# Last convolution group of a streaming encoder chained by channel halves, and one GpSimd scaling moved behind two copies

## What is computed

```python
h = rmsnorm(x, norm_g)
proj = h @ w_in
# attention with band and sinks, gated linear attention (GLA), convolution; each times its gate
u = cv * jax.nn.sigmoid(cgl)
c = conv_lax(concat(conv_hist, u), conv_w) + conv_b            # depthwise, width 31, 256 channels
c = jax.nn.silu(layernorm(c, ln_g, ln_b)) @ w_pw + b_pw
y_conv = c * jax.nn.silu(cg)
y = concat([y_attn, y_gla, y_conv]) @ w_out
return x + y, ...
```

## Time and profile before

| | |
|---|---|
| median of 3 runs | 925.39 us (924.95 to 925.93) |
| profiled execution | 925.71 us, of which the span shown is 923.9 us |
| PE busy | 890.1 us (96% of the span) |
| DVE busy | 784.4 us (85%) |
| ACT busy | 481.6 us (52%) |
| POOL busy | 215.7 us (23%) |
| mean granted TensorE clock | 0.994 |

### The profile page before, as it was taken

How to read it: one execution, slowest core, us unless ns; L and a number is a source line. 1 busy time by engine, 2 the same in 40 slices (tenths; PEclk the granted TensorE clock), 3 DMA queues, 4 the chain that set the end, 5 groups by cost and what they waited for, 6 DMA issues and landing times. The chain is left out here.

```text
span 923.9 us, 15888 instructions
## 1 busy us (share of the span) xinstructions
PE 890.1 (96%) x5655; PEld 800.9 (87%) x5655; DVE 784.4 (85%) x1896; ACT 481.6 (52%) x1182; POOL 215.7 (23%) x259
## 2 busy tenths in 40 slices
PE   6889999999999999998999999999999999999997
PEld 5778888888888888876898888889999899998985
DVE  7898888888888888889879999888788969788994
ACT  7787666666676766668663261341515124142231
POOL 1432222222222222223022231311202012120310
PEclk9999999999999999999999999999999999999999
DMA  9553323222333333135451221121130312204021
GB/s 303 190 191 115 103 82 115 96 110 84 111 106 111 114 115 103 70 120 145 119 160 52 76 69 64 52 81 57 38 101 1 100 39 69 70 3 135 1 81 60
DMA packets 58062, 88.04 MB, mean 95 GB/s; under 512 B 10080, under 2 KB 34528, under 8 KB 57984
## 3 DMA queue, kind: packets, MB, share of 16 engines
q1 hardware_dynamic: 57984, 87.03, 28.8%
HBM read 60.47 MB, written 26.60 MB: 94 GB/s over the span
## 5 line engine op out<-in xcount | busy, mean ns | idle before, releaser
L1826 DVE SCALAR_TENSOR_TENSOR acc<-ub,cwh,acc 128x256 f32<-128x256 f32 (+1 forms) x480 | 230.4, 540 | 1.5 <-ACT acc L1323 0.7
L779 PE MATMUL J<-whi,xhi 128*128 128x512 f32 (+1 forms) x400 | 147.1, 368 | 7.4 <-DVE wlo L489 7.4
L2228 PE MATMUL J<-xbh,whi 128*128 128x256 f32 (+1 forms) x512 | 151.7, 296 | 0.3
L2228 PE MATMUL J<-xbl,whi 128*128 128x256 f32 (+1 forms) x512 | 146.2, 288 | 2.0 <-DVE xbl L587 2.0
L2228 PE MATMUL J<-xbh,wlo 128*128 128x256 f32 (+1 forms) x512 | 147.1, 287 | 0.0
L779 PE MATMUL J<-wlo,xhi 128*128 128x512 f32 (+1 forms) x400 | 143.1, 358 | 0.0
L779 PE MATMUL J<-whi,xlo 128*128 128x512 f32 (+1 forms) x384 | 136.3, 358 | 0.0
L2228 PEld LDWEIGHTS J<-xbh,whi 128*128 128x128 f32 x512 | 98.4, 192 | 2.6 <-DVE wlo L489 1.1
L2228 PEld LDWEIGHTS J<-xbl,whi 128*128 128x128 f32 x512 | 98.2, 192 | 2.2 <-issue 2.2
L2228 PEld LDWEIGHTS J<-xbh,wlo 128*128 128x128 f32 x512 | 98.5, 192 | 0.5
L779 PEld LDWEIGHTS J<-whi,xhi 128*128 128x128 f32 x400 | 76.9, 192 | 16.6 <-issue 7.4
(11 more groups left out here) (287 smaller groups left out, 2233.4 us busy)
## 6 DMA issues: line engine op xcount, KB each, us to landing
out<-res SPq DMA_DIRECT2D x60, 256.0 KB, 2.0
x_normed_scratch<-xraw SPq DMA_DIRECT2D x17, 512.0 KB, 2.9
xtok<-in_x_prompt SPq DMA_DIRECT2D x16, 512.0 KB, 3.6
res<-in_x_prompt SPq DMA_DIRECT2D x16, 512.0 KB, 4.5
xraw<-xT SPq DMA_DIRECT2D x15, 512.0 KB, 3.6
xbraw<-x_normed_scratch SPq DMA_DIRECT2D x14, 512.0 KB, 5.3
res<-out SPq DMA_DIRECT2D x14, 512.0 KB, 3.9
wraw<-in_w_in SPq DMA_DIRECT2D x52, 128.0 KB, 2.5
```

Source lines behind the costliest of these rows:

```text
L779: last = nc.tensor.matmul(bank[:, 0:width], x[x_slot(ps, t)][:, k, :], w, start=(k == 0 and n == 0), stop=(k == KT - 1 and n == len(produc ...
L1826: nc.vector.scalar_tensor_tensor(acc[:, j, 0:frames], src, w, acc[:, j, 0:frames], ALU.mult, ALU.add).then_inc(conv_step, 1)
L2228: last = nc.tensor.matmul(bank[:, 0:w], wt, x[:, k, 0:w], start=(k == 0 and m == 0), stop=(k == KT - 1 and m == 2))
```

## The change

First part, GpSimd in pass A: `norm_x(2)` is no longer called at the end of `body_a(0)`. It is called in `body_a(1)`, behind the two `vdup` copies of tile 1 and ahead of `qk_rinv(2)`. Thereby it stands behind `norm_rinv(3)` too. Nothing else of the order changes.

Second part, the group END only: the chain is cut by channel halves. ScalarE runs affine 0, tanh 0, affine 1, tanh 1. VectorE gates each half alone. TensorE multiplies input half k = 0 into both output halves and then k = 1; output half 0 goes to T[2] and half 1 to the bank S[0], each with a signal of its own. `y_conv` waits for and signals each half, `y_hi` is one operation per half, and `output_end` starts on k = 2 when half 0's high part is there. The order of the steps on VectorE, and on ScalarE apart from the halves, is unchanged.

```diff
+        pw_end = (T[2], S[0])
@@ GpSimd, body_a
                     pool.wait_ge(v_same, 2 * t.n + 2)
+                if t.n == 1:
+                    norm_x(n)
...
-                if t.n >= -1:
+                if t.n >= -1 and t.n != 0:
                     when(t + 2, norm_x)
@@ ScalarE, conv_silu
+                if gi == END:
+                    for j in range(CJ):
+                        nc.scalar.activation(cl[:, j, off:off + w], bank[:, j * 256:j * 256 + w], ACT.Identity,
+                                             scale=convp[:, 1, j:j + 1], bias=convp[:, 2, j:j + 1]).then_inc(cl_ready, 1)
+                        act.wait_ge(cl_ready, 2 * gi + j + 1)
+                        nc.scalar.activation(cth[:, j, off:off + w], cl[:, j, off:off + w], ACT.Tanh, scale=0.5).then_inc(
+                            cth_ready, 1)
+                    return
@@ ScalarE, y_hi
+                if gi == END and dst is ybc:
+                    act.wait_ge(slot_done, SLOT["out", NB - 2, 2 * tiles(NB - 2)[-1] + 1] + 1)
+                    for j in range(CJ):
+                        act.wait_ge(yc_ready, gi + j + 1)
+                        nc.scalar.activation(ybc[:, j, off:off + w], cl[:, j, off:off + w], ACT.Copy, scale=scale).then_inc(
+                            yc_hi, 1)
+                    return
@@ VectorE, y_lo
-                dve.wait_ge(hi, gi + 1)
+                dve.wait_ge(hi, gi + (CJ if gi == END and dst is ybc else 1))
@@ VectorE, conv_gate
+                if gi == END:
+                    for j in range(CJ):
+                        dve.wait_ge(cth_ready, gi + j + 1)
+                        nc.vector.scalar_tensor_tensor(cth[:, j, off:off + w], cth[:, j, off:off + w], 1.0,
+                                                       cl[:, j, off:off + w], ALU.add, ALU.mult).then_inc(cs_ready, 1)
+                    return
@@ VectorE, y_conv
-                dve.wait_ge(pw_psum, gi + 1)
                 dve.wait_ge(gate_done, 4 * b + 4)
+                if gi != END:
+                    dve.wait_ge(pw_psum, gi + 1)
                 for j in range(CJ):
-                    last = nc.vector.scalar_tensor_tensor(cl[:, j, off:off + w], T[2][:, j * 256:j * 256 + w],
+                    if gi == END:
+                        dve.wait_ge(pw_psum, gi + j + 1)
+                    src = pw_end[j][:, 0:w] if gi == END else T[2][:, j * 256:j * 256 + w]
+                    last = nc.vector.scalar_tensor_tensor(cl[:, j, off:off + w], src,
                                                           bpw2[:, j:j + 1], cgate[b % 2][:, j, off:off + w], ALU.add,
                                                           ALU.mult)
-                last.then_inc(yc_ready, 1)
+                    if gi == END or j == CJ - 1:
+                        last.then_inc(yc_ready, 1)
@@ TensorE, output_end
-                pe.wait_ge(yc_hi, groups_before(b + 1))
-                output_half(first, 0, 0, (2, 3), parts=(0, 1))
+                for j in range(CJ):
+                    pe.wait_ge(yc_hi, groups_before(b + 1) + j)
+                    output_half(first, 0, 0, (2 + j,), parts=(0, 1))
@@ TensorE, pointwise
+                    for k in range(CJ):
+                        pe.wait_ge(cs_ready, gi + k + 1)
+                        for j in range(CJ):
+                            last = nc.tensor.matmul(pw_end[j][:, 0:w], wpw[:, k, j * P:(j + 1) * P],
+                                                    cth[:, k, off:off + w], start=(k == 0), stop=(k == CJ - 1),
+                                                    skip_group_check=True)
+                            if k == CJ - 1:
+                                last.then_inc(pw_psum, 1)
+                    return
```

## The result

| | |
|---|---|
| kernel before, measured beside it | 925.55 us median of 21 (923.91 to 926.56) |
| changed kernel | 927.27 us median of 21 (924.11 to 929.33) |
| ratio | 1.0017, 95% interval 1.0011 to 1.0023 |
| predicted | 925.0 us, range 923.2 to 926.2 |

The changed kernel is 1.7 us slower, where a little faster was forecast: the time lies above the range, and the sign is wrong. The difference is just under the 0.2% taken as the bound of "no change". The profiled execution took 927.61 us with a span of 925.8 us, against 925.71 and 923.9.

What follows compares the result with a forecast made beforehand. TensorE, busy 96% of the span, was taken as the bound, so only its pauses or lower clock count. Profiled 925.71 - 0.85 (end) + 0.65 (opening) - 0.15 (clock) = 925.36, 0.3 lower against the median: 925.0 us, range 923.2 to 926.2.

Steps and rivals of the forecast that it cites:

- 6.18 us relay: End, from the affine to TensorE's first output product; cutting it by halves was to start TensorE 0.85 us earlier.
- a start that is earlier by x gives x: End: from 908.89 the chain stays on TensorE until the last addition, so an earlier start counts in full.
- The bounds 0.2 to 1.0: End gain: 0.2 us if only `y_conv`'s earlier start is left, 1.0 if the square and `state` lie as before.
- the third rival: End: the halves bring nothing because fixed times of split operations eat them; 925.7 us, chance 0.10.
- the sum: Opening: scaling holds the last `nmx`, TensorE starts 0.65 us later (0.4 to 1.0), pause grows from 2.44 to 3.1.
- the case I weighed beside the sum: Opening: the small `nmx` gets in first and the scaling holds `sdif` instead; 0.1 to 0.2 us worse.
- The queue: Opening: load of x issued at 68.5 instead of 62.20, first reader at 90.13, so costed at nothing.
- the 0.65 us: Opening: TensorE's later start ahead of tile 0's output matmuls, added in full to the forecast time.
- The clock credit of 0.15 us: Opening: if the lower clock ends at the same moment, a later start spends less in it; 0.15 taken.
- the scaling does no harm: Opening rival: small operations slip through, 923.3 us, or 921.6 without the lower clock; chance 0.15 in all.
- The slower rival: Opening: longer pause brings a second stretch at the lower clock, 1.7 us; 926.9 us, chance 0.07.
- the last sentence of the prediction: Whole kernel: size fails if the lower clock comes or goes at another pause because the program shifts half a microsecond.

Runs made afterwards that it cites:

- end part alone: Chain by channel halves at the end only, with the GpSimd order of the kernel before; 925.09 us, ratio 0.9996; timed again, 926.11 us, 1.0002.
- shifted pair: Unused matmuls in the last block's first cg product: four on end part alone (925.54 us, 1.0000), eight on the changed kernel (926.84 us, 1.0010).
- filled: Seven unused matmuls in TensorE's end pause: added to the changed kernel 925.16 us, ratio 0.9995; added to end part alone 924.70 us, 0.9989.
- with `state` last: Changed kernel with `y_conv` of the last group ahead of `state` on VectorE, 925.04 us, ratio 0.9994; its partner is `state_last`.
- `state_last`: The end part alone, with `y_conv` moved ahead of `state` on VectorE; 924.17 us, ratio 0.9987.
- The pair of profiles above: Two profiles of end part alone, no edit, showing the opening pause, which agrees within 0.03 us between them.
- opening part alone: Kernel before with only GpSimd's scaling of tile 2 moved behind tile 1's copies of v; 925.45 us, ratio 1.0003.

## Why the prediction was wrong

**The end: the shape of the pause was not costed.** This is the step that failed. I treated the 6.18 us relay as pure delay ("a start that is earlier by x gives x") and followed every engine but TensorE's own idle time. My own times contained it: product ready 0.8 us ahead of `y_conv`, output product at 908.04, so a pause from 906.2 to 908.04, 1.84 us, longer than the 1.72 of before. I looked for the clock at the opening only. The price: 1.57 to 1.60 us where the fall comes (five profiles), in 5 of 12 profiles, so 0.7 us on the mean, and the whole 1.6 in the typical execution of the changed kernel, which has it in 3 of 5 profiles.

**The end: the relay, right in kind, 0.24 us short.** 0.61 us instead of 0.85. VectorE's order behaved as forecast (`oss`, `stp`, `y_conv` back to back, `state` holding the ready product). Counted from the affine, `y_conv` starts at 4.43 us instead of 4.29, takes 0.48 instead of 0.45, and TensorE starts 0.66 behind its end (0.09 until `ybc` starts, 0.57 from there), where I had 0.59: the handovers between engines and the fixed times were under-counted, by 0.14, 0.03 and 0.07. `y_conv` gained not 0.2 but 0.07 us (4.43 against the 4.50 of the earlier trace rows). The bounds 0.2 to 1.0 held, and the third rival, that the halves bring nothing, is refuted by every profile.

**The opening: right mechanism, spread under-estimated.** `vcat` at 0.29, the scaling on the last `nmx`, pause 2.99: the sum said 3.1. Over the nine profiles with the moved scaling the pause is 2.97 to 3.67, mean 3.25, against 2.48 in the nine others that have the whole scaling in its old place: +0.77, where I had +0.65 within 0.4 to 1.0. The upper bound failed. In three of nine `sdif` was held for the whole 2.4 us and the pause was 3.64 to 3.67, +1.2. That was the case I weighed beside the sum and priced at 0.1 to 0.2 us. It comes about when the weight piece reaches ScalarE 0.8 to 1.0 us late; when it is later still (1.19 and 1.39) the small operations slip in front and the first weight split is held instead (3.04 and 3.22). I had read ScalarE's wait for that DMA as 0.28 us and took it for fixed. The queue was costed rightly: the load of x was issued at 69.17 us (I had 68.5), and its first reader started at 91.47, as late against 90.13 as TensorE was at that point. The row of the held `sdif` agrees with the exclusion rule of the Trainium skill, SBUF — State Buffer, section Who interferes with whom.

**The opening: whether the delay lasts was not costed.** I passed the 0.65 us on to the end in full. TensorE's start times, compared with the first profile of the end part alone (opening pause 2.49, no fall), show that up to 0.6 us of a delay is taken back by 90 us. With the scaling moved and no fall (one profile, 3.05 us of pause) TensorE is 0.54 us behind at 69 us and level at 90. With the fall the 1.6 us of clock use up what can be taken back: from 64 to 90 us TensorE falls behind by 1.74 us on the mean of eight profiles with the scaling moved and by 0.97 of seven with it in its old place. So, as far as one profile without it can show, the 0.77 counts only in an execution with the fall, which is most of them (8 of 9 with the scaling moved, 7 of 9 with the whole scaling in its old place).

**The clock credit of 0.15 us was wrong.** I had thought of a fall that ends at a fixed moment near 71.5 us. In the changed kernel's profile it began 0.86 us behind the restart and lasted its 3.4 us from there, at the full price of 1.6 us; so it is in 12 of 15 profiles with the whole scaling and a fall there (1.56 to 1.61). Only where it began ahead of the restart, by 0.3 to 0.4 us, was a part of it spent in the pause, and it cost 1.41 to 1.45 (three profiles).

**The range.** Its sum has a slip: the lower bounds of my terms give 924.5, or 924.6 with the credit that I took (-1.0, +0.4, and -0.3 or -0.15 of credit, from 925.39), not 924.3. It changed nothing, since the range went down to 923.2.

**The rivals.** That the scaling does no harm did not happen in any profile. The slower rival named the right cause and a near time (a longer pause costs clock, 926.9), but at the wrong pause: behind the opening pause there is one slow stretch or none, up to 3.67 us, never two. I gave it 0.07 because I tied the fall to one place; the last sentence of the prediction, that a clock that goes at some other pause would upset the size, was where it should have had a chance and a price.

**Does it add up?** From 925.4: -0.61 + 0.77 + 1.6 = 927.2 for an execution with the fall, near the medians of 927.27, 927.16 and 927.01. On means it is less complete. With the fall at 5 in 12, -0.61 + 0.77 + 0.7 = +0.9 us; the 45 executions of the changed kernel average 926.95, 1.5 above the kernel before, so 0.6 us are not accounted for. The end part alone fits (mean of 25: 925.41, no change; -0.61 + 0.7 = +0.1). What the opening part adds on the mean differs by its partner: 0.16 alone, 0.41 in the shifted pair (0.48 of the four further fillers taken off), 0.62 filled, 0.64 with `state` last (each against the kernel before beside it), 1.54 on the end part alone (0.92 where the two were timed side by side). Their average is 0.67 (with the 1.54), near the 0.77 of the pauses; each single one is uncertain by some 0.3 to 0.4. The filled kernels point to where the rest lies: against the kernels before beside them, filling takes the mean of the changed kernel from +1.5 to -0.2 and that of the end part alone from 0.0 to -0.9. At 1.6 us a fall, that would be a fall in about every execution of the one and in about half of the other. Whether the changed kernel really falls more often than the end part alone (3 of 5 against 2 of 5) stays open: profiles are too few, and executions without a profile do not tell where their slow stretches lay.

**A version that is better than both** is `state_last`, 924.17 us, 0.9987 [0.9979, 0.9996] of the kernel before: it takes the relay's gain, another 0.3 us net of the new wait for `on`, and leaves no long pause.

## What to carry to other kernels

When a chain on the critical path is cut into pieces, draw the new idle time of TensorE as well as the new end: a piece that starts earlier but whose successor still waits elsewhere joins two pauses into one, and 0.6 us of relay was paid back with 1.6 us of clock in 5 of 12 profiles. Move what holds the next link first (`state` here, 1.16 us), or keep TensorE busy with unused matmuls. A median over few executions may change by 1 us with no cause in the code when such a fall is a matter of chance (end part alone: 925.09 and 926.11), so ask several profiles how often the slow stretch stands where it costs.

## What the runs showed of the hardware

- The same pause of TensorE is followed by the lower clock in some executions and not in others: 2.0 us at the end in 5 of 12, 2.38 to 3.67 us at the opening in 16 of 19, 1.44 us not in its one profile. The Trainium skill, TensorE: Matmul & The Clock Gate, section Why this matters for your kernels, advises against pauses of TensorE, but names longer ones than those at the end here. Of these, 5 of 12 were followed by the fall, and the measurement decides. The Trainium skill, TensorE: Matmul & The Clock Gate, section What's actually happening, says that the window by which the gate decides runs freely and does not start anew with a kernel. The pair of profiles above agrees: the fall comes 0.3 us ahead of the restart in one and 0.8 behind it in the other.
- A slow stretch costs up to 1.6 us at once, but what is left of it depends on the place. Two profiles of the end part alone both have one at the opening; the one of 925.33 us has three more, near 416, 437 and 525 us, and the one of 926.23 us has none until the end. By TensorE's start times the first stretch puts the one 1.55 us back, and it is all taken back by 430 us; behind the second 0.95 stays; behind the third it is 1.33, and all taken back by 600 us. That another engine is late there anyway would explain it; it was not tested.
- A VectorE operation of 0.17 us can be held for 2.37 us by GpSimd's 2.38 us `tensor_tensor` when it starts 0.03 us behind it (`sdif` in the opening part alone).
